# Front steps dealt out by tile instead of by pair in a decoder layer with expert retrieval

## What is computed

```python
q = (xb @ w_q).reshape(tb, PEER_HEADS, D_KEY)
s1 = jnp.einsum("thd,nd->thn", q[..., :half], k1); s2 = jnp.einsum("thd,nd->thn", q[..., half:], k2)
sc1, i1 = lax.top_k(s1, TOPK); sc2, i2 = lax.top_k(s2, TOPK)
...
top, pos = lax.top_k(cand, TOPK)
g = softmax(top)
act = jax.nn.gelu(jnp.einsum("tnd,td->tn", u_tab[eid], xb), approximate=False)
return jnp.einsum("tn,tnd->td", g * act, v_tab[eid])
```

## Time and profile before

| | |
|---|---|
| runs | 3310.8, 3313.04, 3317.28 us; median 3313.04 |
| profiled execution | 3317.91 us, span 3316.2 us |
| PE, DVE, ACT, POOL busy | 71%, 66%, 30%, 36% of the span |
| mean granted clock of PE | 0.792 |
| read from HBM | 1220.62 MB, of which 1082 MB by POOL's indirect DMAs |

### The profile page before, as it was taken

The page is one execution under the profiler, slowest core; times in us unless marked ns, Lnnn a source line. Parts: engine busy times, 40 slices in busy tenths (PEclk is TensorE's granted clock), DMA queues, the critical chain, the costliest instruction groups (busy, mean ns, idle before and its releaser), DMA issues. The chain is left out here.

```text
span 3316.2 us, 28628 instructions
## 1 busy us (share of the span) xinstructions
PE 2344.2 (71%) x8700; PEld 923.4 (28%) x8700; DVE 2190.7 (66%) x5237; ACT 985.4 (30%) x2525; POOL 1203.9 (36%) x1046
## 2 busy tenths in 40 slices
PE   5998439796989544786969978646465646676665
PEld 4777404342545100232324534200000000010000
DVE  1442895885559979768764568995767574446554
ACT  1111222323233232324242332333233332313422
POOL 0000124442433444445434343444444443425432
PEclk9999769898989667787989989866666675756656
DMA  7552279998999999999999999999999999989998
GB/s 261 208 209 103 90 272 385 404 407 318 419 420 419 412 370 383 417 420 411 411 381 401 418 420 414 410 388 419 421 421 421 421 421 418 421 350 383 422 422 344
DMA packets 201066, 1231.55 MB, mean 371 GB/s; under 512 B 32416, under 2 KB 33056, under 8 KB 68816
## 3 DMA queue, kind: packets, MB, share of 16 engines
q0 software_dynamic: 148608, 1082.20, 79.5%
q1 hardware_dynamic: 52304, 147.53, 11.8%
HBM read 1220.62 MB, written 9.02 MB: 371 GB/s over the span
## 5 line engine op out<-in xcount | busy, mean ns | idle before, releaser
L1139 POOL DMA_INDIRECT big<-in_experts,eid x710 | 834.3, 1175 | 1530.4 <-PE ps L845 1036.8
L1601 DVE SCALAR_TENSOR_TENSOR big<-big,xr 128x1024 f32<-128x1024 f32 x710 | 857.1, 1223 | 519.6 <-DMA big<-in_experts,eid 490.7
L845 PE MATMUL ps<-big,wd 128*32 128x512 f32 x2840 | 789.8, 793 | 548.6 <-ACT wd L1081 538.5
L1079 ACT ACTIVATE wd<-mask,act 128x32 f32<-128x32 f32 x1024 | 328.5, 321 | 1728.7 <-DVE big L1601 1149.5
L612 PE MATMUL ps<-big,wring 128*128 128x384 f32 (+2 forms) x1664 | 561.2, 488 | 16.4 <-DVE arena L1387 10.1
L845 PEld LDWEIGHTS ps<-big,wd 128*32 128x32 f32 x2840 | 102.2, 122 | 1148.4 <-ACT wd L1081 1062.0
L1139 POOL DMA_INDIRECT more_rows<-in_experts,eid x236 | 274.6, 1164 | 391.8 <-PE ps L845 352.7
L845 PE MATMUL ps<-more_rows,wd 128*32 128x512 f32 x944 | 277.0, 812 | 186.1 <-ACT wd L1081 182.1
L1601 DVE SCALAR_TENSOR_TENSOR more_rows<-more_rows,xr 128x1024 f32<-128x1024 f32 x236 | 285.5, 1223 | 171.6 <-DMA more_rows<-in_experts,eid 168.4
L612 PEld LDWEIGHTS ps<-big,wring 128*128 128x128 f32 x1664 | 314.0, 195 | 279.0 <-issue 87.8
L1081 ACT ACTIVATE wd<-wd,gate 128x32 f32<-128x32 f32 x1024 | 329.3, 322 | 33.1
(11 more groups left out here) (244 smaller groups left out, 2089.4 us busy)
## 6 DMA issues: line engine op xcount, KB each, us to landing
wring<-in_w_in SPq DMA_DIRECT2D x67, 512.0 KB
wring<-in_w_q SPq DMA_DIRECT2D x37, 512.0 KB
big<-in_experts,eid POOLq DMA_INDIRECT x710
wring<-in_w_out SPq DMA_DIRECT2D x21, 512.0 KB
wring<-in_w_ada SPq DMA_DIRECT2D x18, 512.0 KB
big<-in_w_ada SPq DMA_DIRECT2D x16, 512.0 KB, 6.8
xr<-in_w_ada SPq DMA_DIRECT2D x14, 512.0 KB, 4.3
wring<-in_w_v SPq DMA_DIRECT2D x11, 512.0 KB
```

The source lines that it names most:

```text
L845: mm = mmul(ps[QUAD * j:QUAD * (j + 1), half, :], wd[:, 2 * (at % 4) + jj, :], values[:, at_h], start=(m == 0), stop=(m == HALF - 1))
L1079: ac(wd[:, c + jj, :], mask[:], ACT.Gelu, scale=act[:, c + jj:c + jj + 1]).then_inc(S["gelu"], 1)
L1139: gp.indirect_dma_start(row(r), None, t["experts"], bass.IndirectOffsetOnAxis(ap=index, axis=0)).then_inc(s_row[r], 16)
L1601: v.scalar_tensor_tensor(out=row(r)[:, 0:D], in0=row(r)[:, 0:D], scalar=1.0, in1=x, op0=ALU.mult, op1=ALU.mult, accum_out=act[:, c:c + 1]) ...
```

## The change

`beside_peer` now treats the two tiles of a pair one by one. Each tile gets half of the pair's steps (the first tile the larger half), on all engines: on ACT and DVE behind the tile's gelu or dot, on PE ahead of the tile's value matmuls. `value`, `gelu` and `dots` become functions of one tile; their bodies, waits and counts are the same. `begin` of PE moves into `value`, `weigh` of DVE directly behind the second dot. `extra` stays behind all of the pair's steps.

```diff
-        def beside_peer(begin, finish, fronts, extra, share=0.0):
+        def beside_peer(tile, fronts, extra, steps_first=False):
             for at in range(NPAIRS):
-                begin(at)
                 n, count = front_steps[at]
-                ahead = min(count, 1 + int(share * count))
-                for _ in range(ahead):
-                    next(fronts[n], None)
-                finish(at)
-                for _ in range(count - ahead):
-                    next(fronts[n], None)
+                for jj in range(2):
+                    if not steps_first:
+                        tile(at, jj)
+                    for _ in range(count // 2 if jj else (count + 1) // 2):
+                        next(fronts[n], None)
+                    if steps_first:
+                        tile(at, jj)
...
-            beside_peer(begin, value, {g.n: front(g) for g in GROUPS[1:]}, lambda at: None, share=0.5)
+            beside_peer(value, {g.n: front(g) for g in GROUPS[1:]}, lambda at: None, steps_first=True)
...
-            beside_peer(gelu, lambda at: None, {g.n: front(g) for g in GROUPS[1:]}, extra)
+            beside_peer(gelu, {g.n: front(g) for g in GROUPS[1:]}, extra)
...
-            def dots(at):
+            def dots(at, jj):
                 b, half, m = place(at)
-                if b is not None and m == 0:
+                if b is not None and m == 0 and jj == 0:
                     dve.wait_ge(S["xr_ready"], 2 * b + half + 1)
-                for jj in range(2):
...
+                if jj == 1:
+                    weigh(at)
...
-            beside_peer(dots, weigh, {g.n: front(g) for g in GROUPS[1:]}, extra)
+            beside_peer(dots, {g.n: front(g) for g in GROUPS[1:]}, extra)
```

More of the change, by code:

```diff
@@ L822, in _, with value @@
                 pass
-            def value(at):
+            def value(at, jj):
                 b, half, m = place(at)
[L828 to L833, removed]
-                for jj in range(2):
[L835 to L847, removed]
@@ new lines, in value @@
+                if jj == 0:
+                    begin(at)
+                    if b is None and m == 0:
+                        pe.wait_ge(S["acc_read"], 2 * (NB - 1) - 1)
+                    elif m == 0 and at == half_start(2 * (NB - 1)):
+                        pe.wait_ge(S["acc_read"], 2 * (NB - 1) + 1)
+                    elif m == 0 and 2 * b + half >= 2:
+                        pe.wait_ge(S["acc_read"], 2 * b + half - 1)
+                values = row(PLAN[at][jj][0])[:, D:2 * D]
+                pe.wait_ge(S["weights"], 2 * at + jj + 1)
@@ new lines, in value @@
+                for h in range(2):
+                    at_h = slice(512 * h, 512 * (h + 1))
+                    if b is None:
+                        k = 2 * m + jj
+                        mm = mmul(ps[QUAD * h:QUAD * h + NS, 0, :], wmask[:, k, :], values[:, at_h],
+                                  start=(k == 0), stop=(k == NS - 1))
+                    else:
+                        j = 2 * h + jj
+                        mm = mmul(ps[QUAD * j:QUAD * (j + 1), half, :], wd[:, 2 * (at % 4) + jj, :], values[:, at_h],
+                                  start=(m == 0), stop=(m == HALF - 1))
@@ L849, in sample_x @@
+                mm.then_inc(S["rows_used"], 1)
             def sample_x(k):
@@ L1062, in _, with gelu @@
                 pass
-            def gelu(at):
+            def gelu(at, jj):
                 b, half, m = place(at)
                 c = 2 * (at % 4)
[L1067 to L1082, removed]
+                if at >= 4 and b is None:
+                    act_.wait_ge(S["rows_used"], 2 * (at - 3))
+                elif at >= 4:
+                    act_.wait_ge(S["rows_used"], 2 * (at - 4) + jj + 1)
+                act_.wait_ge(S["dots"], 2 * at + jj + 1)
+                if b is None:
+                    ac(gel[:, c + jj:c + jj + 1], act[:, c + jj:c + jj + 1], ACT.Gelu).then_inc(S["gelu"], 1)
+                else:
+                    if m == 0 and jj == 0 and half == 0:
+                        g = group_of(b)
+                        act_.wait_ge(*g.to("routes", g.order.index(b - g.blocks[0]) + 1))
+                    ac(wd[:, c + jj, :], mask[:], ACT.Gelu, scale=act[:, c + jj:c + jj + 1]).then_inc(S["gelu"], 1)
+                    act_.wait_ge(S["gelu"], 2 * at + jj + 1)
+                    ac(wd[:, c + jj, :], wd[:, c + jj, :], ACT.Copy,
+                       scale=gate[:, b % 4, 2 * half + jj, m:m + 1]).then_inc(S["weights"], 1)
             def square(n):
@@ L1583, in _ @@
                 pass
-            def dots(at):
+            def dots(at, jj):
                 b, half, m = place(at)
-                if b is not None and m == 0:
+                if b is not None and m == 0 and jj == 0:
                     dve.wait_ge(S["xr_ready"], 2 * b + half + 1)
[L1591 to L1601, removed]
-                                           op0=ALU.mult, op1=ALU.mult, accum_out=act[:, c:c + 1]).then_inc(S["dots"], 1)
+                r, turn, _ = PLAN[at][jj]
+                x = xr[:, 2 * half + jj, :]
+                dve.wait_ge(s_row[r], 16 * (turn + 1))
+                if b is None:
+                    dve.wait_ge(S["xb_mm"], 2 * m + jj + 1)
+                    x = bank2(pair(2 * m + jj))
+                if at >= 4 and jj == 0:
+                    dve.wait_ge(S["gelu"], 2 * (at - 3))
+                c = 2 * (at % 4) + jj
+                v.scalar_tensor_tensor(out=row(r)[:, 0:D], in0=row(r)[:, 0:D], scalar=1.0, in1=x,
+                                       op0=ALU.mult, op1=ALU.mult, accum_out=act[:, c:c + 1]).then_inc(S["dots"], 1)
+                if jj == 1:
+                    weigh(at)
             def weigh(at):
```

## The result

The changed kernel took **3348.57 us** (median of 4 runs, 3345.79 to 3358.6) against 3315.16 for the kernel before (4 runs beside it, 3310.8 to 3318.79): ratio 1.0111, 95% interval [1.0094, 1.0128]. It is **33 us slower** by the medians (37 by the ratio; the two profiled executions lie 30 us apart). The forecast was 3306.6, with a range to 3321: the sign is wrong, and the time lies outside the range. All ratios here compare runs in the fast state; one run of e9 (3506.71 us, granted clock 0.662) was in a slower one and is left out.

A forecast was written before the change was run, and what follows sets the result against it. The DMA, with a ceiling of 421 GB/s, was taken as the bound, leaving 110 us in the front-step stage. Terms -5.8 - 1.6 + 1.2 - 2.7 + 2.5 = -6.4 us from 3313.0 gave 3306.6, range 3290 to 3321.

The forecast's parts named there:

- Full engines: Stretches with PE or DVE full and DMA short: earlier first tiles give -2.7 us at PE, held dots +2.5 at DVE.
- The chain of group 2: Dependent front steps of pairs 55 to 58: the matmul at 796.29 would come 5.8 us earlier.
- The chain of group 3: Dependent front steps of pairs 216 to 219: PE's matmul at 1725.74 would come 1.6 us earlier.
- Pair 0: DVE's mean holds the second dot, so the second tile's dot and gelu delay the root: 1.2 us lost.
- Full DVE: In two DVE-full stretches, such as pair 119, the second dot stands behind a step: +2.5 us together.
- Rival 1: The chain's 5.8 us are given back in the full PE from 800 to 860: 3310 to 3315 us; chance 0.15.
- Rival 2: One late second tile stops all of POOL's fetches behind it: near 3318 or 3329 us; chance 0.18.
- Rival 3: Waits between the halves of PE's steps lower its clock in full stretches: +10 us, 3317; chance 0.05.
- Rival 4: Many small DMA shortfalls close, a quarter of the 110 us: 3286 to 3295 us; chance 0.12.

The follow-up runs named there:

- e9: New order on all engines only in pairs 55-58 and 216-219, PE keeping the old order in 58 and 219, against the kernel before: 3305.25 us, ratio 0.9975.
- e8: New order on all engines in pairs 55 to 58 and 216 to 219 only, against the kernel before: 3308.67 us, ratio 0.9978.
- e1: New order on ACT and DVE only, PE in the order of the kernel before: 3313.88 us, ratio 0.9997 against the kernel before.
- e2: New order on PE only, ACT and DVE in the order of the kernel before: 3342.92 us, ratio 1.0096 against the kernel before.
- e5: Kernel before in its own order, but in 126 split pairs both tiles' value matmuls use the same two PE column groups: 3326.84 us, ratio 1.0034.
- e3: Kernel before in its own order, but in every pair both tiles' value matmuls use the same two PE column groups: 3335.09 us, ratio 1.0064.
- e11: Changed kernel, but PE keeps the old order in the 132 pairs whose two values it would split: 3312.54 us, ratio 1.0005 against the kernel before.
- e4: New order on ACT and DVE, PE doing all steps of a pair before both values: 3317.92 us, ratio 1.0019 against the kernel before.
- e10: New order on all engines only in pairs with 5 or more steps, against the kernel before: 3308.98 us, ratio 0.9984.
- e12: New order on all engines in pairs 230 to 289 only, against the kernel before: 3317.3 us, ratio 1.0007.

## Why the prediction was wrong

- **The step that failed** is in its first sentences on the change: "It adds and removes no operation, DMA or wait", and with it the term *Full engines*, -0.9 for each full stretch of PE. The operations are the same, but their cost isn't: eight value instructions of a pair cost PE 1.06 us together and 2.10 apart. The term was costed only by when a tile is released, and by that "most pairs there have 1 or 2 steps" was a reason for a small number; the pairs with 2 were the ones that paid. In place of the -0.9 at 800 to 820 stands +7.1 (pairs 59 to 72). The forecast's other two stretches, 510 to 560 and the end of 1720 to 1750, show nothing beyond the scatter (0.1 and 1.9 in their rows of the table). "No order makes a full engine faster" is borne out by every run here, but its converse was left out: an order can make a full engine slower.
- **A second step failed with it**: "Where the DMA is full a reordering of engines is hidden". The largest loss, +18.2 in pairs 72 to 120, arose where the DMA had stood at 418 and 419 GB/s and no term was put; PE was as full there as the DMA, and added work took the DMA down to 374 and 363. The +5.8 of 280 to 290 had no term either.
- **It could be seen before.** In the trace of before stand pairs that ACT pulled apart, 53 for one: 750.66 and 752.51, four instructions in 1.05 us each, where eight took 1.06 a few us ahead (742.62). The forecast read count and length of the steps (L612) from such rows, not of the values.

```profile
750.66 1.05 PE L845 MATMUL ps<-big,wd 128*32 128x512 f32 x4
752.51 1.05 PE L845 MATMUL ps<-big,wd 128*32 128x512 f32 x4 [0.80 <-ACT wd L1081]
```

- **The chain of group 2** was right in its mechanism: -5.8 forecast, -6.0 in the changed kernel at the first dot of pair 59, -5.8 in e8 and e9. The length it was stated for, some 31 us, is 29.45 in the changed kernel, and a term that the forecast did not have stands in it: PE's two matmul groups in the chain, mean and variance. They took 9.46 us before (granted clock 0.57 from 764 to 770), 2.85 + 4.54 in the changed kernel (1.00 from 763 to 767) and 5.46 + 5.42 in e1 (0.50 from 764 to 770):

```profile
764.85 5.46 PE L726 MATMUL ps<-arena,onesm 128*128 128x384 f32 x8 [1.63 <-DVE mbuf L1369]
...
775.44 5.42 PE L736 MATMUL ps<-arena,onesm 128*128 128x384 f32 x8 [4.07 <-ACT arena L992]
...
794.91 5.49 PE L617 MATMUL ps<-big,wring 128*128 128x384 f32 x8 [0.93 <-DVE arena L1392]
```

From the first dot of pair 55 to the first matmul of the next projection, less these two groups, the traces have 27.1 us before, 26.4 in e2 and e5, 26.3 in e3, and 21.0 in e1, e8 and e9 (22.1 in the changed kernel). So the order of ACT and DVE gives 5.4 to 6.1 us by itself, and PE's order nothing: e2's -2.7 stands in e3 and e5 too, which have the order of before and a mean of 2.82 us. e1 and e11 have only -3.6 and -3.5 because PE ran the two groups more slowly.

- **The chain of group 3**: -1.6 forecast, -1.5 in e8 and -2.6 in e9, within the scatter of one trace; in the changed kernel it is +1.9, with split pairs in the same stretch.
- **Pair 0**: +1.2 forecast, +1.0 at the first dot of pair 1, and the root at 435.40 in place of 434.44. The table has 1.0 for each kernel whose ACT and DVE have the new order in pair 0, and 0.0 for each other.
- **Full DVE** (+2.5 for two stretches): at pair 119 nothing of it is seen, the first dots of pairs 119 to 124 keep their distances to 0.1 us. At 2160 to 2240 there is a sign of it: from pair 290 to 320 the four kernels with the new order on DVE there (after, e1, e4, e11) have 1.6 or 1.7 us, the nine others 0.1 to 1.1.
- **Rival 1**, hidden, with "PE's full stretch begins at 796.29 because the chain ends there" against it: e8 bears the argument out: 5.8 us are won ahead of the full stretch, 0.5 lost in it, and the rest is still there at pair 320.
- **Rival 2**, the second tile is held: its sign came true by luck. The reason it gives is worth some 6 us in e4, and e10, which has the new order in pairs 71, 82, 128 and 235, is faster than before. Its chance of 0.18 was not a forecast of what happened.
- **Rival 3**, PE's clock: the mean granted clock rose, 0.80 against 0.79, with PE busier. From 800 to 820 and from 1000 to 1050 it is 1.00 in both kernels.
- **Rival 4**, smoother everywhere: it wanted over 402 GB/s in the stage of the front steps; the stage has 390, down from 396.
- **The range** held no case in which an engine's work grows.

The Trainium skill (TensorE: Matmul & The Clock Gate, Part 3: Packing small matmuls) says that small matmuls placed in different 32 x 32 tiles of the array run concurrently, and that the output's group of 32 PSUM partitions is the column tile. This case's traces agree: 1.06 us for both tiles in four groups (845.30, before), 1.91 in two (1049.34, e5).

**What stays open.** How much of the loss on a full PE is its added work alone: e5, with 0.85 us of it a pair and no change of order, loses 11 us, PE's order alone (e2) 32. The 0.32 us a pair between them, the room r and the some 6 us of a held tile can make up the rest, but no run separates them.

## What to carry to other kernels

Before an edit that "only moves" work, look at what stands next to what on each engine: two neighbours may overlap, and the row of the pair costs less than two rows of the single. Compare count and length of a group's rows in the timeline (8 in 1.06 us, 4 in 1.05), and keep such neighbours together, above all where that engine is full. An order that pays in a chain of dependent steps and costs on a full engine belongs in the few pairs of the chain: e9 has it in 8 pairs of 516 on ACT and DVE, in 6 of them on PE, and wins 0.25%; everywhere it loses 1.1%. When you compare a chain's length between kernels, first take out the matmul groups whose time follows the clock: here that turned lengths of 29.7 to 33.9 us (e1, e2, e3, e5 and e8) into two values, 21.0 and 26.4.

## What the runs showed of the hardware

- Value matmuls of one tile (128 x 32 weights, 512 columns, fp32, two column groups) took 1.05 us, those of two tiles in four groups 1.06, those of two tiles in the same two groups 1.91, all at the full granted clock.
- Added PE work stayed hidden under a full DMA for as long as PE had room: in e12's trace nothing up to pair 280, then 3.5 us within ten pairs.
- The mean's 8 matmul instructions took 2.85 us at a granted clock of 1.00 (763.63, changed kernel, PE busy up to there) and 4.97 at 0.57 (behind 3.91 us of idle time, before): the extra work on PE shortened a chain of other engines by 2.1 us.
- A run of 16 instructions of the steps (L612) took 5.36 us up to the next group's start; cut in two by a value group, its halves took 2.78 each (846.29 before, 841.91 and 845.67 after).
